# A streaming-encoder layer on eight cores: mixer-output and residual transposes moved from TensorE to DMA

## Time and profile before

| | us |
|---|---|
| median of 3 runs | 3258.37 |
| lowest, highest run | 3254.9, 3886.76 |
| profiled execution | 3283.31 |
| its span (slowest core, core 5) | 3281.8 |
| span of core 0 in it | 3231.4 |
| TensorE busy on core 5 | 3168.4 (97%) |
| VectorE, ScalarE, GpSimd busy on core 5 | 1876.3 (57%), 1185.6 (36%), 681.9 (21%) |
| share of the 16 DMA engines' time, core 5 | 54.6% |

### The profile page before, as it was taken

The page is one execution under the profiler, slowest core; times in us unless marked ns, Lnnn a source line. Parts: engine busy times, 40 slices in busy tenths (PEclk is TensorE's granted clock), DMA queues, the critical chain, the costliest instruction groups (busy, mean ns, idle before and its releaser), DMA issues.

```text
span 3281.8 us, 48876 instructions; the slowest of 8 cores (3231.4 to 3281.8 us)
## 1 busy us (share of the span) xinstructions
PE 3168.4 (97%) x16592; PEld 1511.0 (46%) x16592; DVE 1876.3 (57%) x3799; ACT 1185.6 (36%) x1837; POOL 681.9 (21%) x635
## 2 busy tenths in 40 slices
PE   4899998999999999999999999999999999999998
PEld 2444443444444444444444444444444444444444
DVE  3856656646556474564736656375564745647444
ACT  4563535233233332333324233342333323332233
POOL 1512102302213121131302213022130211313001
PEclk9899998999999999999999999999999999999999
DMA  9757755545546464464645546455464644645442
GB/s 275 240 194 249 255 191 195 210 152 199 186 172 214 147 220 167 166 224 155 219 154 180 199 161 221 160 183 202 169 208 149 217 164 177 218 154 187 149 170 86
DMA packets 113858, 618.31 MB, mean 188 GB/s; under 512 B 13136, under 2 KB 13392, under 8 KB 63440
## 3 DMA queue, kind: packets, MB, share of 16 engines
q1 hardware_dynamic: 113616, 615.19, 54.6%
HBM read 554.32 MB, written 60.82 MB: 187 GB/s over the span
## 4 chain that ended last, share of the span: by engine, by line
PE 94%; DMA 2%; ACT 1%; DVE 1%; issue 1%; SPq 1%; POOL 0%; DVEq 0%; ACTq 0%; POOLq 0%
PE ps L621 89%; PE ps L629 3%; DMA stage<-wf 2%; SPq L502 1%; ACT rel L1048 0%; PE ps L936 0%; PE ps L768 0%; PE ps L804 0%; PE ps L816 0%; PE ps L806 0%; ACT scr L927 0%; DVE TG L884 0%; ACT ring L577 0%; ACT ring L588 0%; DMA xb<-x 0%
## 5 line engine op out<-in xcount | busy, mean ns | idle before, releaser
L621 PE MATMUL ps<-TG,ring 128*128 128x512 bf16 x5120 | 1188.4, 386 | 56.2 <-ACT ring L577 39.3
L621 PE MATMUL ps<-ring,TG 128*128 128x512 bf16 x4096 | 984.0, 385 | 20.7 <-ACT rel L1048 10.7
L621 PE MATMUL ps<-ring,hT 128*128 128x512 bf16 x4096 | 926.7, 380 | 0.0
L621 PEld LDWEIGHTS ps<-TG,ring 128*128 128x128 bf16 x5120 | 501.0, 99 | 655.4 <-issue 140.1
L621 PEld LDWEIGHTS ps<-ring,TG 128*128 128x128 bf16 x4096 | 399.5, 99 | 498.6 <-issue 90.0
L1052 DVE TENSOR_TENSOR hT<-rel 128x512 bf16<-128x512 f32 x457 | 374.6, 820 | 420.8 <-ACT rel L1048 418.1
L621 PEld LDWEIGHTS ps<-ring,hT 128*128 128x128 bf16 x4096 | 395.4, 98 | 449.6 <-issue 11.7
L1048 ACT ACTIVATE rel<-ps 128x512 f32<-128x512 f32 x512 | 304.8, 596 | 755.3 <-PE ps L621 749.6
L1075 DVE SCALAR_TENSOR_TENSOR xb<-ps,st,xb 128x512 f32<-128x512 f32 x288 | 215.3, 747 | 275.6 <-PE ps L621 274.6
L724 POOL TENSOR_TENSOR qk<-scr 128x512 bf16<-128x512 f32 x128 | 163.8, 1280 | 873.7 <-DVE scr L721 873.7
L636 ACT ACTIVATE xsb<-xb 128x1024 bf16<-128x1024 f32 x200 | 210.5, 1052 | 330.2 <-DVE xb L1075 231.3
(11 more groups left out here) (79 smaller groups left out, 2379.0 us busy)
## 6 DMA issues: line engine op xcount, KB each, us to landing
ring<-wb SPq DMA_DIRECT2D x366, 1024.0 KB, 5.5
stage<-wf SPq DMA_DIRECT2D x104, 512.0 KB, 8.1
stage<-xT SPq DMA_DIRECT2D x64, 512.0 KB, 7.4
xb<-x SPq DMA_DIRECT2D x64, 512.0 KB, 5.5
out<-xb SPq DMA_DIRECT2D x64, 512.0 KB, 3.7
stage<-x SPq DMA_DIRECT2D x56, 512.0 KB, 10.8
wb<-ring SPq DMA_DIRECT2D x26, 1024.0 KB, 9.3
rot<-ROT SPq DMA_DIRECT2D x16, 512.0 KB, 6.1
```

Of the source, the lines that this page charges most:

```text
L621: r = e.matmul(out(), lhs(k), rhs(k), start=(start + k == 0), stop=(start + k == total - 1))
```

## The change

From tile 3 on, `yT` no longer transposes by TensorE: each 128x512 half (131,072 bytes) is moved by one transposing DMA on SyncE's queue from its y buffer straight into `ymix`. `norm_T` does the same with 128x1024 blocks (262,144 bytes) into `N2T[t]` for t >= 3, and into `n3` for t = 2 to 14. The PSUM bank and the copy of each fall away there. A transposing DMA counts for the planner as 1.3 us of SyncE and 3.74 times its bytes, and is due 3 us of plan time earlier than the transposes were. The planner holds back any DMA while more than 6 us of DMA work is queued (`DMA_AHEAD`). The pool `xsb` grows from 2 to 4 buffers, `scr` shrinks from 9 to 8 and `st` from 16 to 14. In `norm_T` the thrown-away squares now go into the same `xsb` buffer that the cast writes next. As the planner runs over the whole graph, the lists of all engines are made anew.

```diff
--- before.py
+++ after.py
@@ -130,6 +130,7 @@
 
 
 DMA_BW = 265e3
+DMA_AHEAD = 6.0
 
 
 def list_schedule(g):
@@ -193,6 +194,9 @@
                     if op.ready > now + 1e-9:
                         continue
                     if e in op.lock and port[0] > now + 1e-9:
+                        continue
+                    if op.dma is not None and dma_free[0] > now + DMA_AHEAD:
+                        heapq.heappush(events, dma_free[0] - DMA_AHEAD)
                         continue
                     if not can_alloc(op, now):
                         continue
@@ -405,8 +409,8 @@
 
 TINY = 0.16
 TILE = 196.0
-KN_NSLOT = dict(ring=6, TG=3, x=8, hT=16, qk=8, v=4, svn=2, ktok=2, PT=2, y=8, xsb=2, pT=1, stage=4,
-                rot=1, rel=3, gt=2, scr=9, st=16, psum=8, Sbf=2)
+KN_NSLOT = dict(ring=6, TG=3, x=8, hT=16, qk=8, v=4, svn=2, ktok=2, PT=2, y=8, xsb=4, pT=1, stage=4,
+                rot=1, rel=3, gt=2, scr=8, st=14, psum=8, Sbf=2)
 
 
 def build(nseq):
@@ -630,9 +634,14 @@
                 return r
             return {"pe": (n * MS, fn)}
 
-        def sqsum(xbuf, acc, racc, vt):
-
-            j = g.buf("xsb")
+        def dmaT(out, in_, reads, writes, vt, key, nbytes):
+
+            g.add({"sp": (1.3, lambda e: e.dma_start_transpose(out=out(), in_=in_()))}, reads, writes, vt, dma=key,
+                  nbytes=nbytes * 3.74)
+
+        def sqsum(xbuf, acc, racc, vt, j=None):
+
+            j = g.buf("xsb") if j is None else j
             g.add({"act": (t_act(1024) + 0.19, lambda e: e.activation(out=ap(j), in_=ap(xbuf), func=AF.Square,
                                                                      accum_out=acc()))},
                   [(xbuf, 0), (xbuf, 1)], [(j, 0), racc], vt)
@@ -876,6 +885,10 @@
             ymix = g.buf("TG")
 
             def yT(b, half, src):
+                if t >= 3:
+                    dmaT(lambda: ap(ymix)[:, 4 * half:4 * half + 4, b * 128:(b + 1) * 128], lambda: ap(src),
+                         [(src, 0)], [(ymix, (half, b))], vt[0] - 3, lambda: ("ty", src.slot), 131072)
+                    return
                 p = g.buf("psum")
                 g.add(transposes(p, lambda k: ap(src)[:, k * 128:(k + 1) * 128], 4), [(src, 0), c("ident")], [(p, 0)],
                       vt[0])
@@ -998,7 +1011,7 @@
                             if b == 0:
                                 N2T[t] = g.buf("TG")
                                 INV2[t] = g.buf("st")
-                            norm_T(t, b, N2T[t], INV2[t], vt[0])
+                            norm_T(t, b, N2T[t], INV2[t], vt[0], t >= 3)
                             adv(8 * MS)
             for t in ts:
                 s4 = INV2[t]
@@ -1008,14 +1021,18 @@
                 g.add({"dve": (TINY, lambda e, s4=s4: e.reciprocal(out=stc(s4, 8, 4), in_=stc(s4, 4, 4)))},
                       [(s4, "ms")], [(s4, "inv")], vt[0])
 
-        def norm_T(t, b, dst, stb, vt):
+        def norm_T(t, b, dst, stb, vt, by_dma):
 
             xx = X[t, b]
-            sqsum(xx, lambda: stc(stb, b), (stb, ("ss", b)), vt)
             xs = g.buf("xsb")
+            sqsum(xx, lambda: stc(stb, b), (stb, ("ss", b)), vt, xs)
             g.add(both(1024, lambda e: e.tensor_copy(out=ap(xs), in_=ap(xx)),
                        lambda e: e.activation(out=ap(xs), in_=ap(xx), func=AF.Copy)),
                   [(xx, 0), (xx, 1)], [(xs, 0)], vt, lock=("dve",))
+            if by_dma:
+                dmaT(lambda: ap(dst)[:, :, b * 128:(b + 1) * 128], lambda: ap(xs), [(xs, 0)], [(dst, b)], vt - 3,
+                     lambda: ("tx", xs.slot), 262144)
+                return
             p = g.buf("psum")
             g.add(transposes(p, lambda k: ap(xs)[:, k * 128:(k + 1) * 128], 8), [(xs, 0), c("ident")], [(p, 0)], vt)
             o_ = lambda: ap(dst)[:, :, b * 128:(b + 1) * 128]
@@ -1095,7 +1112,7 @@
             n3 = g.buf("TG")
             st = g.buf("st")
             for b in range(NB):
-                norm_T(t, b, n3, st, vt[0])
+                norm_T(t, b, n3, st, vt[0], 2 <= t < NT - 1)
                 adv(8 * MS)
             g.add({"dve": (TINY, lambda e: e.tensor_scalar(out=stc(st, 4, 4), in0=stc(st, 0, 4), scalar1=1.0 / D,
                                                           scalar2=EPS, op0=ALU.mult, op1=ALU.add))},
```

## The result

Against the kernel before on the same chip the changed one takes 0.9621 of the time (95% interval 0.9561 to 0.9681), and in a second comparison, on another chip, 0.9644 (0.9628 to 0.9659). That is 123 us by the first and 115 us by the second. The changed kernel's median is 3133.55 us, where 3163 was forecast with a range from 3145 to 3300. Several medians, of the kernel before above all, contain runs in which one die was slower; the ratios leave those out, so what follows goes by ratios.

What follows compares the result with a forecast made beforehand. TensorE was taken to set the pace (94% of the chain). Transposes -68.6, waits -30, additions +2 and +1.5 sum to -95.1 us; from the median 3258.4 that gives 3163 us, range 3145 to 3300.

Steps and rivals of the forecast that it cites:

- Bounds: 0 ... and 33.3; I take 30 us: TensorE's short waits at the mixers' ends, tiles 3 to 14: they go, saving 30 us, at most 33.3.
- only reorders: 0: Cap on queued DMA: keeps a transpose from standing behind several 1 MB loads, worth 0 us.
- The additions of +2 and +1.5 us: +2 us at the last gate, where the cast must follow the square; +1.5 us for residual late arrivals.
- The price of a transposing DMA: DMA time per 128 KB: estimated 1.8 us, between 0.85 and 19; no cost to TensorE up to the plan's 1.85.
- engine load, 147 of 190 us in a tile: DMA engines per tile: 43 us of transposes beside 104 us of present load, 147 of 190 us, which fits.
- Rival 3: Slower: TensorE stands at outproj and gate for the transposes, from 2.6 us per 128 KB on; chance 0.18.
- 208 us for each us of lateness: Late data at outproj and gate: 16 units per tile, 13 tiles, 208 us per us of excess; 0 taken.
- That hides some us of delay: 0: SyncE's queue: weight loads behind transposes are covered by six ring buffers, about 45 us of matmuls; cost 0.
- Rivals 1 and 2: 1: PSUM waits return as waits for late y, 3190 to 3205, chance 0.10; 2: late data spend gain, 3195 to 3323, 0.21.

Runs made afterwards that it cites:

- the run with the residual alone: Changed kernel with the mixer's outputs transposed on TensorE again, only the residual's transposes by DMA (832 fewer): ratio 0.9834 to the kernel before.
- ymix first: Kernel before, all transposes on TensorE, loads of the transposed input ordered after ymix gets its TG buffer, tiles 3 on: ratio 0.9865.
- y alone: Changed kernel with the residual's transposes back on TensorE, only the mixer's outputs by DMA (416 fewer): ratio 0.9770 to the kernel before.
- the cheap plan: Changed kernel, planner reckoning a transposing DMA at 0.1 us of SyncE and a tenth of its bytes: ratio 0.9638 to the kernel before.
- two pieces: Changed kernel with each transposing DMA issued as two halves, the plan not told: ratio 0.9823 to the kernel before, 58 us slower than the changed kernel.
- single pieces: Changed kernel with each transposing DMA issued as 4 or 8 128x128 pieces, plan not told: ratio 1.1923 to the kernel before.

## Why the prediction was wrong, step by step

**The direction and the mechanisms held.** TensorE was the bound, and each transpose taken away gave its 55 to 56 ns (70 us for 1248; the tile of the run with the residual alone bears it out). The burst of waiting y was the cause of the waits. Two runs show it that have only this in common, that y does not stand in PSUM waiting for a buffer: with ymix first all copies stay, with y alone n1T keeps its turn.

**The step that failed: "Bounds: 0 ... and 33.3; I take 30 us".** This is the term for the waits that should go. It was mis-sized, and measured about 42 us: 3.49 us per tile by the tile's length in the run with ymix first, and 44 and 43 us by the ratios of that run and the run with y alone. The prediction took the column of idle time. That column counts from a matmul's recorded end, and a small matmul's record is 0.219 us long where the next may start after 0.056. The starts tell the loss. Four lines of the kernel before, core 0, beside those of the earlier trace rows:

```profile
1425.79 0.39 PE L936 MATMUL ps<-svn,wsTb 128*128 128x128 bf16 x4
...
1428.61 0.39 PE L629 MATMUL ps<-ident,y 128*128 128x128 bf16 x4
1429.61 1.89 PE L621 MATMUL ps<-TG,ring 128*128 128x512 bf16 x8 [0.61 <-ACT rel L1048]
1432.34 1.89 PE L621 MATMUL ps<-ring,TG 128*128 128x512 bf16 x8 [0.84 <-ACT rel L1048]
```

Four small matmuls from 1425.79 on are over, in sequence, at 1426.01; the next starts at 1426.89: 0.88 us lost where the idle column says 0.71. The four waits of a mixer are 0.88, 0.78, 1.00 and 0.83, 3.49 us instead of 2.84, the same 3.49 by which the tile got shorter with ymix first. Twelve mixers make 42 us. Starts had been used for the transposes and not for the waits; with 42 for 30 the sum would have been 3151.

**The cap "only reorders: 0"** was wrong too. It was costed where transposes stand behind loads and not at the start, where TensorE waits for its first weights and the queue is the path. It is worth 4 to 14 us alone; beside the rest it is 5 or 13 us, not clear of noise by the times, and 8.5 us by the first transposes of k. The start was in the trace: 37.4 us on core 0, 39.15 on core 1, with 4 MB of x ahead of the weights.

**The additions of +2 and +1.5 us** did not show: 1.000 for the buffers and the shared square, no wait for TG. Together, with 7 us for the cap (between the 9 alone and the 5 beside the rest): -70 - 42 - 7 = -119 instead of -95.1; measured are 115 and 123. That is also why the range missed: with all waits gone and nothing added the prediction's own bounds reach 3156.5, its lower end of 3145 left 11 us for the unknown, and the waits passed their bound of 33.3 by 9 us and the cap took 5 to 9 more.

**The price of a transposing DMA.** The prediction took 1.8 us per 128 KB between 0.85 and 19. 128 KB more take 3.1 - 2.5 = 0.6 us, and one issue holds SyncE for 1.23 us at either size, so a burst moves one half per 1.27 us. The lower end was nearer, and it made no difference, as the prediction said of prices under 1.85. The Trainium skill (Advanced Engine Details and Errata, X-Bar Transpose (TRN2)) calls such DMAs as fast as regular ones. The data part roughly agrees: 0.6 us for 128 KB more, where a plain load of 1024 KB lands 2.2 us later than a plain store of 512 KB, 0.55 us per 128 KB (core 1). The issue does not: 1.23 us, where plain DMAs took from 0.33. Nor does the DMA engines' time: on core 1 their busy time rose from 1810 us (55.9% of 3238.6) to 2033 us (65.1% of 3122.7), which is 0.71 us for each of 312 units of 128 KB, where the plain DMAs before took 0.39 us on average (an estimate from these shares, which takes the plain DMAs' time for unchanged). The prediction's engine load, 147 of 190 us in a tile, was too high all the same: 68% of 188.4 us is 128. The Trainium skill's 1309 ns for a 128x128 block (VectorE: DVE Perf Modes, The three transpose paths) does not add up over the blocks of one DMA here: four more blocks took 0.6 us. Rival 3, slower from 2.6 us per 128 KB on, fell with that.

**208 us for each us of lateness** was wrong. It counted every us of lateness as a wait and left out what the order leaves between landing and first use. With the cheap plan lateness cost nothing; with two pieces 58 us where 190 were put down. In the changed kernel the fifth half, with which outproj's first block is complete (the four YR come first in the program), lands at about 1402 (1394.40 + 4 x 1.27 + 2.5) and is used at 1406.47: some 4.5 us of lateness are covered there. In the two-piece run it lands at about 1028.7 (1014.59 + 9 x 1.29 + 2.5), and outproj starts at 1029.06, late. The gate has more room (in the changed kernel its first block lands at about 1459.7, 1456.63 + 3.1, and is used at 1470.79) and waits in neither. With single pieces, at +740 us, a large cost did come, through the queue that the weights share: the prediction's "That hides some us of delay: 0" holds for 20 us of issue in a tile, no longer wholly for the 40 of two pieces (9.6 us of waits for weights), and not for 115.

Rivals 1 and 2 are refuted by the middle stretch, where TensorE does not wait.

## What to carry to other kernels

When a wait of an in-order engine is to be priced, take the distance between starts, with the pipelined work subtracted, and not the idle column; for TensorE here that was 3.49 against 2.84 us per tile. The length of a tile, from one operation to the same one some tiles later, checks such a price to 0.1 us. When copies out of PSUM come in a burst long after their matmuls, look for the destination buffer that is missing: an order of buffers alone brought 44 us. And follow a change of a queue's order to the start of the kernel, where no other work hides it.

## What the runs showed of the hardware

- Issuing a transposing DMA held SyncE's queue for 1.20 to 1.23 us (medians) at 32, 64, 128 and 256 KB alike; plain DMAs took from 0.33 us. Cut into 1248 pieces instead of 208, the same transposes made the kernel 19% slower than before. The pieces themselves landed in 2.3 us, and the DMA engines were less busy (52.2% on core 1, against 65.1%): what cost was the issue.
- With 40.8 MB more moved, the DMA engines' share rose from 54.6% to 64.9% on the slowest core. All of the 166,400 packets that came with the transposes are under 512 bytes.
- Weight loads landed 0.5 us later on core 1 (6.4 against 5.9) and 0.8 us on core 0 (6.2 against 5.4). That the transposes are the cause is not shown: with the cap alone it was 6.0 on core 0 and 5.5 on core 1.
